# Attention layers: the upper weights of 56 projection blocks multiply both input parts in one 512-column product

## The reference

```
h = rms_norm(x, pre_norm_g[l]) * (1.0 + scale[:, None, :]) + shift[:, None, :]
proj = h @ w_in[l]                       # 1024 -> 4096 columns
q, k, v, g_att = proj[..., 0:512], [512:1024], [1024:1536], [1536:2048]
u, b_gate, c_gate, g_conv = proj[..., 2048:2560], ...
att = dilated_attention(q, k, v, rel_bias) * silu(g_att)
cnv = b_gate * short_conv(c_gate * u, conv_w[l]) * silu(g_conv)
mix = concatenate([att, cnv], axis=-1) @ w_out[l]
x = x + gate[:, None, :] * rms_norm(mix, post_norm_g[l])
```

## Time and profile before

| | |
|---|---|
| Time, 3 runs | 786.64 us median (785.78 to 786.76) |
| The profiled execution's own time | 786.75 us |
| Its span (first to last instruction) | 784.8 us |
| TensorE busy | 775.0 us (99%) |
| VectorE / ScalarE / GpSimd busy | 579.6 / 415.3 / 117.5 us |
| Granted TensorE clock, mean | 0.998 |
| Layer 0: first qk block to last g block | 537.8 to 629.8 us |
| Layer 1: the same | about 127.5 us later |

### The profile page before, as it was taken

The page is one execution under the profiler, slowest core; times in us unless marked ns, Lnnn a source line. Parts: engine busy times, 40 slices in busy tenths (PEclk is TensorE's granted clock), DMA queues, the critical chain, the costliest instruction groups (busy, mean ns, idle before and its releaser), DMA issues.

```text
span 784.8 us, 14582 instructions
## 1 busy us (share of the span) xinstructions
PE 775.0 (99%) x5764; PEld 731.9 (93%) x5764; DVE 579.6 (74%) x926; ACT 415.3 (53%) x731; POOL 117.5 (15%) x136
## 2 busy tenths in 40 slices
PE   9999999999999999999999999999999999999997
PEld 9999999999899999889999998879999988999985
DVE  6777777799596976678777787977677768567763
ACT  7544444445257566485444443456655557455541
POOL 3800000033230000000000000010064411035510
PEclk9999999999999999999999999999999999999999
DMA  9877666695416644378766769555474571754531
GB/s 341 303 262 245 218 234 247 212 332 208 149 60 214 219 149 144 124 266 308 280 243 219 258 222 372 187 191 187 139 240 134 162 263 37 244 181 133 156 116 53
DMA packets 46114, 161.93 MB, mean 206 GB/s; under 512 B 5168, under 2 KB 6736, under 8 KB 46048
## 3 DMA queue, kind: packets, MB, share of 16 engines
q1 hardware_dynamic: 46048, 161.01, 59.2%
HBM read 159.91 MB, written 1.08 MB: 205 GB/s over the span
## 4 chain that ended last, share of the span: by engine, by line
PE 89%; DVE 4%; DMA 4%; issue 1%; ACT 1%; SPq 0%; POOL 0%; DVEq 0%; POOLq 0%; ACTq 0%
PE ps L367 23%; PE ps L369 22%; PE ps L368 22%; PE ps L756 3%; PE ps L814 3%; PE ps L816 3%; PE ps L815 3%; DMA adr<-wada 2%; DVE w L1230 2%; DMA raw<-wst 1%; PE ps L671 1%; PE ps L615 1%; PE ps L746 1%; PE ps L727 1%; PE ps L736 1%
## 5 line engine op out<-in xcount | busy, mean ns | idle before, releaser
L1230 DVE TENSOR_TENSOR w<-raw,w 128x1024 fp32r<-128x1024 f32 x237 | 287.6, 1222 | 127.5 <-ACT w L867 127.0
L367 PE MATMUL ps<-u,w 128*128 128x256 f32 (+1 forms) x1275 | 364.6, 286 | 0.2 <-DVE w L1230 0.2
L369 PE MATMUL ps<-u,w 128*128 128x256 f32 (+1 forms) x1275 | 360.0, 282 | 0.0
L368 PE MATMUL ps<-u,w 128*128 128x256 f32 (+1 forms) x1275 | 359.7, 282 | 0.0
L867 ACT CAST w<-raw 128x1024 fp32r<-128x1024 f32 x237 | 246.1, 1049 | 115.8 <-PE ps L369 82.8
L367 PEld LDWEIGHTS ps<-u,w 128*128 128x128 f32 x1275 | 239.3, 188 | 5.1 <-issue 3.1
L369 PEld LDWEIGHTS ps<-u,w 128*128 128x128 f32 x1275 | 239.6, 188 | 0.0
L368 PEld LDWEIGHTS ps<-u,w 128*128 128x128 f32 x1275 | 239.4, 188 | 0.1
L1248 DVE SCALAR_TENSOR_TENSOR acc<-adr,cact,acc 128x1024 f32<-128x1024 f32 x42 | 55.6, 1341 | 5.5 <-DMA adr<-wada 5.4
L1929 POOL TENSOR_SCALAR Sb<-Sb,st 128x256 f32<-128x256 f32 x32 | 45.1, 1425 | 95.5 <-DVE st L1698 95.5
L911 ACT ACTIVATE si<-tmp 128x272 f32<-128x272 f32 (+1 forms) x40 | 17.0, 425 | 66.1 <-DVE tmp L1343 66.1
(11 more groups left out here) (269 smaller groups left out, 978.1 us busy)
## 6 DMA issues: line engine op xcount, KB each, us to landing
raw<-wst SPq DMA_DIRECT2D x245, 512.0 KB, 4.4
adr<-wada SPq DMA_DIRECT2D x48, 512.0 KB, 3.9
Bt<-bias_rows SPq DMA_DIRECT2D x8, 192.0 KB, 4.1
hT<-xT SPq DMA_DIRECT2D x4, 272.0 KB, 4.7
sq<-nrow SPq DMA_DIRECT2D x2, 512.0 KB, 4.8
g2row<-weight_rows SPq DMA_DIRECT2D x2, 512.0 KB, 5.9
sq<-weight_rows SPq DMA_DIRECT2D x2, 512.0 KB, 5.1
outT<-hT SPq DMA_DIRECT2D x4, 256.0 KB, 2.0
```

Of the source, the lines that this page charges most:

```text
L367: e.matmul(out, a, x1, start=first, stop=False)
L368: e.matmul(out, a, x2, start=False, stop=False)
L369: return e.matmul(out, b, x1, start=False, stop=last)
L1230: e.tensor_tensor(b, r, a.bitcast(F32), ALU.subtract).then_inc(*tick(s_split, k))
```

## The change

`u1` and `u2` become the two halves of one tile `u12`. For the 8 qk and 20 g blocks of each layer `wide_block` replaces `block`: per step the upper weights multiply both parts in one product of 512 columns (line 392 after), which goes to the whole bank, upper input to columns 0 to 255 and lower input to columns 256 to 511; the lower weights still multiply the upper input in one product of 256 columns (line 393), onto the first half. The two halves have to be added when the bank is read. ScalarE copies the second half to a new tile `lo_` with three places ("low", `lower_half`). For qk, POOL subtracts the upper part from it, and VectorE adds the first half. For g, VectorE adds both halves, and what read the bank before now reads the sum, the tanh too. The cast of qk's upper part still reads the first half alone.

```
-        u1 = sb("u1", [P, KT, TP], F32R)
-        u2 = sb("u2", [P, KT, TP], F32R)
+        u12 = sb("u12", [P, 2, KT, TP], F32R)
+        u1, u2 = u12[:, 0, :, :], u12[:, 1, :, :]
...
+            def wide_block(key, c):
+                e.wait_ge(s_split.handle, c + 1)
+                b = place(key)
+                both = ps[:, b, :].rearrange("p (h q) -> p h q", h=2)
+                for kt in range(KT):
+                    hi, lo = (w[:, kt * P:kt * P + P] for w in PLACE[c])
+                    if kt < KT - 1:
+                        e.matmul(both, hi, u12[:, :, kt, NMETA:T], start=kt == 0, stop=False, skip_group_check=True)
+                    m = e.matmul(ps[:, b, 0:S], lo, u1[:, kt, NMETA:T], start=False, stop=False, skip_group_check=True)
+                    if kt == KT - 1:
+                        m = e.matmul(both, hi, u12[:, :, kt, NMETA:T], start=False, stop=True, skip_group_check=True)
...
-                    block(("qk", l, j), C_QK[l] + j, x1, x2, S)
+                    wide_block(("qk", l, j), C_QK[l] + j)
...
-                        block(("g", l, i), C_G[l] + i, x1, x2, S)
+                        wide_block(("g", l, i), C_G[l] + i)
... ScalarE
                 def tanh_of(key, before):
-                    proj(key)
+                    e.wait_ge(*read(key))
                     if before:
-                        e.wait_ge(*read(before))
-                    e.activation(cw_[l][:, 4, :], out_of(key), ACT.Tanh, scale=0.5).then_inc(*tick(s_tanh, key))
+                        e.wait_ge(s_use.handle, at(s_use, before))
+                    e.activation(cw_[l][:, 4, :], lo_[l][:, key[2] % 3, :], ACT.Tanh, scale=0.5).then_inc(*tick(s_tanh, key))
+
+                def lower_half(key, j, free):
+                    b = bank_of(key)
+                    if free:
+                        e.wait_ge(*free)
+                    flip = key[0] == "qk" and j < 4
+                    e.copy(lo_[l][:, j % 3, :], ps[:, b, 2 * S - 1:S - 1:-1] if flip else ps[:, b, S:2 * S]).then_inc(
+                        *tick(s_low, key))
...
                     e.copy(qk[l][:, j, :], ps[:, b, S - 1::-1] if j < 4 else ps[:, b, 0:S]).then_inc(*tick(s_qk1, (l, j)))
+                    lower_half(("qk", l, j), j, read(("qk", l, j - 3)) if j > 2 else None)
...
+                    proj(key)
+                    lower_half(key, i, used(i - 3) if i > 2 else read(("qk", l, (6, 7, 5)[i])))
                     if i < 4 or p_ == 3:
                         tanh_of(key, before)
                         before = key
-                    elif p_ == 0:
-                        proj(key)
-                        if k > 1:
-                            e.wait_ge(*read(("g", l, i - 3)))
-                        e.copy(cw_[l][:, 0, :], out_of(key)).then_inc(*reading(key))
... VectorE
-                    e.wait_ge(s_qk1.handle, at(s_qk1, (l, j)))
-                    e.tensor_tensor(qk2[l][:, j, :], ps[:, b, S - 1::-1] if j < 4 else ps[:, b, 0:S], qk[l][:, j, :].bitcast(F32),
-                                    ALU.subtract).then_inc(*reading(("qk", l, j)))
+                    e.wait_ge(s_dif.handle, at(s_dif, (l, j)))
+                    e.tensor_tensor(qk2[l][:, j, :], ps[:, b, S - 1::-1] if j < 4 else ps[:, b, 0:S], lo_[l][:, j % 3, :],
+                                    ALU.add).then_inc(*reading(("qk", l, j)))
...
+                    x = lo_[l][:, i % 3, :]
+                    e.wait_ge(s_low.handle, at(s_low, key))
+                    if i > 3 and p_ == 0:
+                        e.tensor_tensor(cw_[l][:, 0, :], out_of(key), x, ALU.add).then_inc(*reading(key))
+                        continue
+                    e.tensor_tensor(x, out_of(key), x, ALU.add).then_inc(*reading(key))
                     if i < 4:
                         e.wait_ge(s_tanh.handle, at(s_tanh, key))
-                        e.scalar_tensor_tensor(sg[l][:, i, :], cw_[l][:, 4, :], 1.0, out_of(key), ALU.add,
-                                               ALU.mult).then_inc(*reading(key))
+                        e.scalar_tensor_tensor(sg[l][:, i, :], cw_[l][:, 4, :], 1.0, x, ALU.add,
+                                               ALU.mult).then_inc(*tick(s_use, key))
... POOL
+                for j in range(8):
+                    x = lo_[l][:, j % 3, :]
+                    e.wait_ge(s_low.handle, at(s_low, ("qk", l, j)))
+                    e.tensor_tensor(x, x, qk[l][:, j, :].bitcast(F32), ALU.subtract).then_inc(*tick(s_dif, (l, j)))
```

More of the change, by code:

```diff
@@ L188, in build @@
         qk2 = []
-        qk, Vt, sg, Sb, PT, st_, at_, cu, cw_, m1, m2 = ([] for _ in range(11))
+        qk, Vt, sg, Sb, PT, st_, at_, cu, cw_, m1, m2, lo_ = ([] for _ in range(12))
         for l in range(2):
@@ L209, in build @@
                 side.append(sb("side1", [P, 3, 2, CH], F32R, lx))
+            lo_.append(sb(f"low{l}", [P, 3, S], F32, lx) if l == 0 else lo_[0])
             lx.close()
@@ L873, in out_of, with low_of @@
                 return ps[:, bank_of(key), 0:n]
+            def low_of(key):
+                return ps[:, bank_of(key), S:2 * S]
             def first_input():
@@ L1043, in tanh_of, with used @@
                 def tanh_of(key, before):
-                    proj(key)
+                    e.wait_ge(*read(key))
                     if before:
-                        e.wait_ge(*read(before))
-                    e.activation(cw_[l][:, 4, :], out_of(key), ACT.Tanh, scale=0.5).then_inc(*tick(s_tanh, key))
+                        e.wait_ge(s_use.handle, at(s_use, before))
[7 more added lines that the diff above has]
+                        *tick(s_low, key))
+                def used(i):
+                    key = ("g", l, i)
+                    return read(key) if i > 3 and i % 4 == 0 else (s_use.handle, at(s_use, key))
                 def split_mix(k, src):
@@ L1724, in attention @@
                     if p_ == 1:
-                        proj(key)
-                        e.wait_ge(*read(("g", l, i - 1)))
-                        e.tensor_tensor(cu[l][:, 1:S + 1], cw_[l][:, 0, :], out_of(key), ALU.mult).then_inc(*reading(key))
                         e.wait_ge(*read(key))
+                        e.tensor_tensor(cu[l][:, 1:S + 1], cw_[l][:, 0, :], x, ALU.mult).then_inc(*tick(s_use, key))
+                        e.wait_ge(s_use.handle, at(s_use, key))
                         e.tensor_scalar(cw_[l][:, 1, :], cu[l][:, 0:S], tap_of(l, 0, j), None, ALU.mult).then_inc(
@@ L1739, in attention @@
                             e.wait_ge(s_m2.handle, at(s_m2, (l, 4 + j - 1)))
-                        e.scalar_tensor_tensor(cw_[l][:, 2, :], cw_[l][:, 1, :], 0.5, out_of(key), ALU.mult,
-                                               ALU.mult).then_inc(*reading(key))
+                        e.scalar_tensor_tensor(cw_[l][:, 2, :], cw_[l][:, 1, :], 0.5, x, ALU.mult,
+                                               ALU.mult).then_inc(*tick(s_use, key))
                     elif p_ == 3:
@@ L1745, in attention @@
                         e.wait_ge(s_tanh.handle, at(s_tanh, key))
-                        e.scalar_tensor_tensor(cw_[l][:, 3, :], cw_[l][:, 4, :], 1.0, out_of(key), ALU.add,
-                                               ALU.mult).then_inc(*reading(key))
+                        e.scalar_tensor_tensor(cw_[l][:, 3, :], cw_[l][:, 4, :], 1.0, x, ALU.add,
+                                               ALU.mult).then_inc(*tick(s_use, key))
             def weighed_rows(s, t, hf):
@@ L1945, in attention @@
                     if 4 <= i < 20 and p_ == 3:
-                        e.wait_ge(*read(("g", l, i)))
+                        e.wait_ge(s_use.handle, at(s_use, ("g", l, i)))
                         e.tensor_tensor(cw_[l][:, 2, :], cw_[l][:, 2, :], cw_[l][:, 3, :], ALU.mult).then_inc(
```

6 lines of the change are left out of this document (5 added, 1 removed).

## The result

| | before | after |
|---|---|---|
| Time, median of 4 runs each on one chip | 786.50 us (785.78 to 786.76) | 810.56 us (808.61 to 813.04) |
| Ratio | | 1.0301, 95% interval 1.0278 to 1.0324 |
| The profiled execution's own time | 786.75 us | 811.62 us |
| Its span | 784.8 us | 809.7 us |
| Granted TensorE clock, mean | 0.998 | 0.993 |

The change costs 24.1 us. It was forecast to cost 17.1, and the range ended at 808.5: the direction and the mechanism came as written, the size did not. TensorE's clock, which the forecast put at nothing, and several terms of its walk, each a little too small, make up the difference.

What follows compares the result with a forecast made beforehand. TensorE, busy 775.0 of 784.8 us, was the bound, a slower ScalarE-VectorE loop hidden by a 3.3 us lead. Layers 0 and 1 add 8.8 and 8.3, +17.1 on 786.75: 803.85, median 803.7; range 796 to 808.5.

Steps and rivals of the forecast that it cites:

- The rival on the clock: TensorE's clock falls to 1.2 GHz in the new waits; whole rounds at that clock would give 875 us; chance 2%.
- the walk: Step-by-step timing of layer 0, also used for layer 1: +8.8 us in layer 0, +8.3 in layer 1.
- the loop: ScalarE and VectorE pass work to and fro in the g blocks; round 14.97 us against TensorE's 14.51 before the change.
- A turn in g 0 to 3: Weight cast, split, addition, then tanh in series in the first four g blocks: 2.91 us, against TensorE's 2.76 a block.
- The saving of the wide product: TensorE's step in query, key and g blocks falls from 353.4 to 344.5 ns: 3.95 us over 56 blocks.
- The query and key blocks' new chain: Cast, lower-half copy, POOL's difference, VectorE's addition: 0.93 us later per block; TensorE 0.56 earlier; pair 0's scores at 562.04.
- Blocks g 0 to 3: First four g blocks: three serial turns of 2.91 us put the fourth tanh at 577.30, next scores at 578.04 against 574.46.
- The rounds: Four g blocks each, on VectorE: 1.61 us longer, from 14.67 and 14.97 to 16.28, 16.58 and 16.58 us.
- Behind layer 0: After layer 0's last block: 0.7 us stall for a bank, 0.5 us more for the last weight split.
- TensorE stays the bound: Rival for the whole kernel: TensorE's saving reaches the end, 782.7 us; chance 4%.
- The tanh's round trip is soaked up: Rival in the g blocks: first four keep TensorE's pace, a round grows only 0.76 us; 790.4 us; chance 8%.
- The wide product is no cheaper: Rival on TensorE's products: query and key blocks' 1.1 us saving goes, 804.8 us; inside the forecast, no separate chance.

Runs made afterwards that it cites:

- e6: Kernel after with products whose result nothing reads ahead of each transpose that waits (12, and 22 ahead of the last): 807.32 us, ratio 1.0254.
- e5: Kernel after run once more, unchanged, beside the kernel before: 810.13 us, ratio 1.0295.
- e3: Kernel before with u1 and u2 as halves of one tile u12, nothing else changed: 786.59 us, ratio 0.9998.
- e1: Kernel before with u12 and the wide product, old evacuation reading only the bank's first half, so the lower-input product is left out: 785.56 us, ratio 0.9987.
- e2: Kernel after with three products of 256 columns per step instead of the wide product, new evacuation kept: 809.46 us, ratio 1.0284.
- e7: e1 with the two input parts of a step 320 columns apart in the tile instead of 2560: 785.65 us, ratio 0.9983.
- e8: Kernel after with the change only in the 16 query and key blocks, the 40 g blocks as before: 786.12 us, ratio 0.9986.
- e4: Kernel after with, in g blocks with a tanh, the lower-half copy ahead of the weight cast and the addition ahead of the weight split: 796.68 us, ratio 1.0117.
- e10: e4 with g blocks p_ = 1 and 2 from block 4 on narrow again, 40 of 56 blocks wide: 788.94 us, ratio 1.0029.

## Why the prediction was right in kind and short in size

**The step that failed: the clock was put at nothing.** The sum has no term for it. The rival on the clock was priced as all or nothing, 875 us at 2%, from whole rounds at 1.2 GHz, and the argument against it was that waits near 2.5 us lie between dense blocks. The runs show a case in between that had no place in the sum. The clock falls behind some of the waits and then comes back: in the kernel after for some three microseconds each behind 3.33 us of idle time at 631.37, 2.16 at 753.65 and 1.91 at 770.63, not behind 1.87, 1.85 and 2.13 in layer 0. e6 against e5 puts the cost at 2.8 us. Forecast and clock together, 803.7 + 2.8 = 806.5, lie inside the range. What carried the time over its end are another 4.0 us, by which the terms of the walk were too small. Either alone would have stayed inside.

**Where the time went.** The distances between a few starts on TensorE take the kernel apart: the first query/key product of each layer, its last transposes (head 7), its first output product. Besides those already shown, three starts each of the kernel before, the kernel after and e6, from their timelines:

```profile
665.40 0.28 PE L367 MATMUL ps<-u,w 128*128 128x256 f32 x1
747.23 0.60 PE L736 MATMUL ps<-cs,Sb 128*128 128x128 f32 x4
757.36 0.39 PE L814 MATMUL ps<-w,m 128*128 128x512 f32 x1
...
540.04 0.40 PE L392 MATMUL ps<-u,w 128*128 128x512 f32 x1
679.25 0.40 PE L392 MATMUL ps<-u,w 128*128 128x512 f32 x1
782.29 0.39 PE L832 MATMUL ps<-w,m 128*128 128x512 f32 x1
...
537.10 0.39 PE L392 MATMUL ps<-u,w 128*128 128x512 f32 x1
638.56 0.39 PE L836 MATMUL ps<-w,m 128*128 128x512 f32 x1
777.21 0.39 PE L836 MATMUL ps<-w,m 128*128 128x512 f32 x1
```

In the table, the forecast is the kernel before with the terms of the forecast added.

| Stretch, us | before | forecast | e6 | after | e5 |
|---|---|---|---|---|---|
| Layer 0, first query/key product to last transposes | 82.07 | 89.87 | 91.36 | 91.33 | 91.32 |
| from there to the first output product | 9.97 | 9.75 | 10.10 | 11.38 | 12.76 |
| from there to layer 1's first query/key product | 35.58 | 36.78 | 37.17 | 36.50 | 36.36 |
| Layer 1, first query/key product to last transposes | 81.83 | 89.63 | 91.37 | 91.38 | 91.37 |
| from there to the first output product | 10.13 | 9.91 | 10.11 | 11.66 | 12.51 |
| from there to the end of the span | 27.44 | 28.14 | 27.99 | 27.41 | 27.39 |
| Sum | 247.0 | 264.1 | 268.1 | 269.7 | 271.7 |

Up to the last transposes the three executions agree within 0.05 us, whatever the clock does: there the loop sets the pace, and what a slow TensorE loses is taken out of its next wait. Behind the last transposes there is no such wait, and there the clock shows: 1.3 and 1.6 us in the kernel after, 2.7 and 2.4 in e5, of which the stretches behind the layers give some back. In all it costs 1.6 us in the one execution and 3.6 in the other, on either side of the 2.8 between the medians. e6 against the forecast, 268.1 against 264.1, is the 4.0 us of the walk: 3.2 in the two stretches of the loop, 0.5 behind the last transposes, 0.2 behind the layers.

Another 2.3 us of the 24.9 between the two spans arise ahead of the layers, where the change touches nothing but the tile's layout: the first query/key product starts at 537.78 before and at 540.04 after, at 539.89 in e5, 539.39 in e3, 537.34 in e1, 537.10 in e6 and 536.73 in e2. All but the first of these have the tile, so it does not explain them. The change itself is worth 22.6 us in the profiled execution.

**What the terms measured.** e6 is used for layer 0, since its clock does not fall.

| Step of the forecast | forecast | measured |
|---|---|---|
| TensorE's step, ns | 344.5 | 350 |
| First query/key product to scores of pair 0 | 24.26 | 24.73 |
| A turn in g 0 to 3 | 2.91 | 2.98 |
| Scores of pair 0 to scores of pair 1 | 16.00 | 16.30 |
| First round | 16.28 | 16.46 |
| Second round | 16.58 | 16.85 |
| Last transposes to first output product | 9.75 | 10.10 |

- *The saving of the wide product* was mis-sized, 3.95 us forecast, 1.3 us measured. Steps alternate as the timeline of the kernel after shows:

```profile
540.40 0.40 PE L392 MATMUL ps<-u,w 128*128 128x512 f32 x1
540.63 0.28 PE L393 MATMUL ps<-u,w 128*128 128x256 f32 x1
540.75 0.39 PE L392 MATMUL ps<-u,w 128*128 128x512 f32 x1
```

  A step here is 350 ns: the 512 columns take 0.23 us, where the earlier trace rows have 226.7 ns, and the 256 columns 0.12. ScalarE's casts of qk, one to a block, give the period over whole blocks:

```profile
554.36 0.38 ACT L1099 CAST qk<-ps 128x256 fp32r<-128x256 f32 x1 [1.22 <-PE ps L395]
...
562.77 0.37 ACT L1099 CAST qk<-ps 128x256 fp32r<-128x256 f32 x1 [1.20 <-PE ps L395]
```

  Three periods, 2.803 us each. Before it was 8 x 353.4 = 2.827 by the earlier trace rows. That is 0.024 us a block, 1.3 us in 56. Of the 8.9 ns that a 512-column product took less than two of 256 columns among products of its own kind, 5.5 are not saved beside a 256-column one. Why is open; e7 shows that it is not the strips' distance. The Trainium skill's 2.5 ns of fixed cost ("TensorE: Matmul & The Clock Gate", section "Wait — 56ns, not 53.3ns?") had given an estimated 1.1 us, near the measurement, though what a product takes above its columns at 2.4 GHz is 11 and 13 ns in the earlier trace rows and 15 ns in the alternating steps (350 against 320 ns for two). This term moved the end by 0.8 us at most, since only the query and key blocks' share reaches it.
- *The query and key blocks' new chain* was right within 0.1 us: 1.03 us later where 0.93 was forecast. But TensorE came only 0.19 us earlier, not 0.56, so the scores of pair 0 were 0.47 later than forecast, counted from the layer's first product. That they start at 561.83 in e6, beside a forecast of 562.04, is luck: this execution reached the layer 0.68 us earlier than the kernel before. In e8 no product of the layers waits for another engine.
- *Blocks g 0 to 3* took 0.30 us longer than forecast, most of it in three turns of 2.98 instead of 2.91.
- *The rounds* were 0.2 to 0.3 us longer each than forecast. Two terms are seen in the tile `low` of the kernel after (min/median/max ns):

```profile
L1068 ACT ACTIVATE cw<-low x16: 416/417/419, 571.3 to 783.7; 128x256 f32<-128x256 f32 x16
...
L1766 DVE TENSOR_TENSOR cu<-cw,low x8: 426/426/428, 589.3 to 776.5; 128x256 f32<-128x256 f32 x8
```

  The multiplications that now read SBUF were credited with 0.07 each. They take 426 ns, where the one from the bank took 410, so twice 0.07 comes back; and the tanh takes 417 from SBUF against 383 from the bank. That is 0.17 of the rounds' excess of 0.18 and 0.27. With the two points above, and a third round like the second, the excess makes the last transposes of the layer 1.5 us later than forecast. Another 0.35 comes in the three blocks behind them, which were taken 0.2 shorter than before and are not.
- *Behind layer 0* the bank stall was 0.28 us instead of 0.7, the wait for the last weight split 0.72 instead of 0.5. The stretch grew by 1.6 us, and the 0.6 left of it are not resolved.

In layer 1 the same stretch of the loop grew by 9.5 us, where the forecast took over 7.8 from layer 0. Forecast, walk and clock come to 17.1 + 4.0 + 2.8 = 23.9 of the 24.1 us. That it fits so closely is partly luck: the executions reach the layers at times 3 us apart.

**The rivals.** "TensorE stays the bound" is refuted by the chain and by e2, where taking away TensorE's saving changed nothing that shows. "The tanh's round trip is soaked up" is refuted by the rounds of 16.5 and 16.8, and e4 shows what it would have needed: the addition ahead of the split. "The wide product is no cheaper" was nearer for this term than the 3.95 us, and its 1.1 us lay inside the range.

**What was right.** The forecast's reading was that a closed loop between two engines, each far from full, was already as slow as TensorE's round, and that a lead of 3.3 us hid it. The experiments bear it out: a longer loop costs time once the lead is spent (e2, e4, e10), a shorter TensorE then gives nothing that shows (the change against e2), and with the loop left as it was (e1, e7, e8) no transposes wait. What is not separated is how much of the longer loop is the additions and how much ScalarE's copies.

## What to carry to other kernels

Before work is moved from the busiest engine to one with spare time, measure the distance between two like instructions on the receiving engine over one round, not its busy share. If work passes to and fro between two engines, an operation between them costs its duration and its handovers, and its place in the written order may matter more than its size: here the order gave 13 us at equal work, the clock's share included. And price the clock as several short losses behind single waits, not as all or nothing: only those count that no later wait swallows.

## What the runs showed of the hardware

- The clock falls inside an otherwise dense kernel. After single waits of TensorE of 2.2 and 3.3 us it stood at 1.2 GHz for some three microseconds; in the same execution waits of 1.85 and 2.13 us left it at 2.4 GHz, and one of 1.91 us at 770.63 did not. In e5, the same program, it fell behind 1.86 us at 721.48, where the kernel after kept it, and it stayed down longer, to 637.0 behind the 3.33 us that end at 631.21. So the length of the last wait alone does not decide. The Trainium skill ("TensorE: Matmul & The Clock Gate", section "HAM oscillation — how this bites in real kernels") tells of a clock that falls at every repeated wait for a DMA between short bursts of products. Here single waits for ScalarE between longer dense stretches were enough, and not each of them.
- Reading SBUF instead of PSUM was not cheaper. On ScalarE the tanh of 128x256 went from 383 to 417 ns, on VectorE an operation with two inputs from 410 to 426 ns. The Trainium skill ("VectorE: DVE Perf Modes", section "The TRN2 errata — SBUF-src ops pay a fixed extra latency per instruction") has ScalarE's fixed part 52 cycles longer from SBUF, an estimated 43 ns at the 1.2 GHz it gives; this case's 34 ns agree in sign and roughly in size. For VectorE its table has SBUF cheaper, and here the measurement decides against it; but of the two inputs before, one was already in SBUF. The same section's formula for an fp32 addition of two tensors, (N + 151) / 0.96 ns, gives an estimated 424 ns for 256 columns, and there the 426 ns agree.
- A 512-column product took 9 ns less than two of 256 columns when the neighbours were alike, and about 3 ns less between 256-column products.
- In the profiled execution of the kernel after, products of 272 columns ahead of the layers ran at a pace of 126.7 ns instead of 125.4, about the 2.3 us by which it reached the layers later. e5, the same program, and e3 had 125.4, so it belongs to that one execution, and its cause is open. e5 was as late for other reasons, so such a delay does not need this pace.
